# Latent attention: where the two short groups of context queries stand in each set of heads

## The reference, cut to what matters

```
def block_attention(q, k, v, scale):
    ...
    def one_block(qi):
        s = jnp.einsum('bhqd,bhkd->bhqk', qi, k).astype(jnp.float32) * scale
        p = jax.nn.softmax(s, axis=-1).astype(v.dtype)
        return jnp.einsum('bhqk,bhkd->bhqd', p, v)
...
a_lat = block_attention(qa_l, jnp.concatenate([ka_c, ka_l], axis=2), jnp.concatenate([va_c, va_l], axis=2), scale)
...
y_ctx = combine(block_attention(qa_c, ka_c, va_c, scale), h_c, mo_c, z_c, u_ctx.dtype)
```

## Time and profile before

| | |
|---|---|
| median of 3 executions | 4053.97 us (4051.37 to 4055.36) |
| profiled execution, its own time | 4052.3 us |
| its span | 4050.5 us |
| mean granted TensorE clock | 0.989 |
| TensorE busy | 3951.8 us (98%) |
| VectorE, ScalarE, GpSimd busy | 44%, 24%, 21% |
| the attention, first score maximum to last output | 304.22 to 674.16 us |
| first instruction of the next stage on TensorE | 674.95 us |

### The profile page before, as it was taken

The page is one execution under the profiler, slowest core; times in us unless marked ns, Lnnn a source line. Parts: engine busy times, 40 slices in busy tenths (PEclk is TensorE's granted clock), DMA queues, the critical chain, the costliest instruction groups (busy, mean ns, idle before and its releaser), DMA issues. The chain is left out here.

```text
span 4050.5 us, 48141 instructions
## 1 busy us (share of the span) xinstructions
PE 3951.8 (98%) x18490; PEld 2440.7 (60%) x18490; DVE 1775.2 (44%) x3770; ACT 957.0 (24%) x1802; POOL 835.2 (21%) x911
## 2 busy tenths in 40 slices
PE   7999999999999999989999999999999999999998
PEld 4688886877558468567544565656544444444447
DVE  3227775577333366646356322222523252223134
ACT  4223332333114311155225311111111010000001
POOL 0006665101111111132012112123100022111223
PEclk8999999999999999999999999999999999999999
DMA  5320003110202121132131112113243101111113
GB/s 212 125 91 8 8 9 64 47 44 34 102 28 77 50 63 48 58 109 94 47 95 50 57 36 80 41 57 104 94 184 104 52 32 42 42 42 48 46 42 104
DMA packets 113571, 270.24 MB, mean 67 GB/s; under 512 B 15479, under 2 KB 45033, under 8 KB 112254
## 3 DMA queue, kind: packets, MB, share of 16 engines
q1 hardware_dynamic: 106368, 251.81, 18.8%
q0 software_dynamic: 5920, 13.25, 1.4%
q10 hardware_dynamic: 1056, 2.10, 0.1%
HBM read 218.53 MB, written 50.87 MB: 67 GB/s over the span
## 5 line engine op out<-in xcount | busy, mean ns | idle before, releaser
L426 PE MATMUL upper_banks<-sbuf 128*128 128x512 f32 (+1 forms) x2016 | 771.4, 545 | 1.5 <-issue 1.1
L3152 PE MATMUL upper_banks<-sbuf 128*128 128x512 f32 x1400 | 614.6, 595 | 5.6 <-ACT sbuf L3411 3.9
L426 PEld LDWEIGHTS upper_banks<-sbuf 128*128 128x128 f32 x2016 | 382.4, 190 | 388.7 <-issue 374.2
L3152 PEld LDWEIGHTS upper_banks<-sbuf 128*128 128x128 f32 x1400 | 262.7, 191 | 316.5 <-issue 307.0
L2417 PE MATMUL gla_prod<-sbuf 128*128 128x512 f32 x560 | 247.6, 593 | 0.3 <-DVE sbuf L2449 0.3
L378 POOL TENSOR_TENSOR sbuf<-sbuf 128x512 f32<-128x512 f32 x36 | 47.7, 1325 | 901.8 <-POOLq L68 330.0
L582 DVE TENSOR_TENSOR sbuf<-upper_banks,sbuf 128x512 f32<-128x512 f32 (+1 forms) x140 | 81.9, 585 | 283.1 <-PE upper_banks L426 282.6
L1007 PE MATMUL mla_banks<-sbuf 128*128 128x128 f32 x1344 | 175.2, 279 | 12.1 <-DVE sbuf L1314 8.5
L2417 PEld LDWEIGHTS gla_prod<-sbuf 128*128 128x128 f32 x560 | 104.5, 192 | 119.9 <-issue 117.4
L1007 PEld LDWEIGHTS mla_banks<-sbuf 128*128 128x128 f32 x1344 | 162.7, 194 | 21.8 <-issue 11.6
L1627 PE MATMUL mls_banks<-sbuf 128*128 128x512 f32 x392 | 175.1, 593 | 0.0
(11 more groups left out here) (535 smaller groups left out, 6497.2 us busy)
## 6 DMA issues: line engine op xcount, KB each, us to landing
sbuf<-in_l_w_in SPq DMA_DIRECT2D x59, 512.0 KB, 4.0
sbuf<-in_w_in SPq DMA_DIRECT2D x52, 512.0 KB, 4.4
sbuf<-in_w_mlp_out SPq DMA_DIRECT2D x40, 512.0 KB, 3.6
sbuf<-in_w_mlp_in SPq DMA_DIRECT2D x32, 512.0 KB, 3.6
sbuf<-in_l_w_mod SPq DMA_DIRECT2D x24, 512.0 KB, 5.2
scratch_gates<-sbuf SPq DMA_DIRECT2D x48, 256.0 KB, 2.0
sbuf<-scratch_gates SPq DMA_DIRECT2D x8, 1536.0 KB, 6.8
sbuf<-in_l_w_mod SPq DMA_DIRECT2D x8, 1024.0 KB, 15.3
```

Source lines behind the costliest of these rows:

```text
L426: last = nc.tensor.matmul(bank_of(n, c)[:, 0:wd], lw[:, k * P:(k + 1) * P], right_operand(c, base, tw, k, o, wd, to), start=k == 0 and c i ...
L3152: last = nc.tensor.matmul(pb, lw[:, k * P:(k + 1) * P], rhs, start=k == 0 and c in ("P1", "P2", "P5"), stop=k == 3, skip_group_check=True)
```

## The change

In each of the first three sets the order of query tiles becomes 2 3 4 0 5 6 7 1 8 9; in the last it becomes 2 3 4 0 5 6 7 8 9 1. Before it was 2 to 9 and then 0 and 1 in all four. The number of groups, their content and all formulas for waits stay; those that count by the group's kind (`nkt`, `adds`) follow the list.

```
-    groups = [(j, t) for j in range(4) for t in list(range(2, TT)) + [0, 1]]
+    groups = [(j, t) for j in range(4) for t in ((2, 3, 4, 0, 5, 6, 7, 1, 8, 9) if j < 3 else (2, 3, 4, 0, 5, 6, 7, 8, 9, 1))]
```

## The result

The changed kernel takes 4076.05 us (median of 6, 4073.26 to 4082.04), the kernel before 4052.67 us in the same comparison (median of 6, 4049.48 to 4055.36). Ratio 1.0059, 95% interval 1.0046 to 1.0072: 23.4 us slower. The forecast was 4073, slower, between 4064 and 4081.

What follows compares the result with a forecast made beforehand. Long groups were taken as bound by TensorE's work plus small waits, nearly matched by GpSimd's two-group chain, with GpSimd ending last in the first short group. 4052.3 + 16.1 + 3.0 = 4071.4, 4073 against the median; range 4064 to 4081.

Steps and rivals of the forecast that it cites:

- Long to short: First layer's attention: time from a long group's first VectorE score maximum to the next short group's, claimed to stay 8.82 us.
- Short to long: First layer's attention: time from a lone short group's first VectorE score maximum to the next long group's, claimed 10.40 us.
- The long step behind: First layer's attention: step from the long group after a lone short one to the next long group, claimed 9.57 us.
- The sum at equal clock: First layer's attention, first marker to end, without new clock falls: 386.02 us against 369.94, claimed +16.1 us.
- The end: First layer's attention, from the last group's marker to the stage's end: claimed 11.78 us with one short group there.
- The mechanism: Inside a lone short group, GpSimd's key sums for the long neighbour hide its work; it costs 9.60 us, like a long one.
- The clock: TensorE in lone short groups: one in three falls to the lower clock, two falls of 1.52 us, claimed +3.0 us.
- clock falls at most of the places: Rival for TensorE at the seven lone short groups: five to seven falls of 1.52 us, 4076 to 4079 us, chance 0.20.
- The signs of being wrong: Short-to-long step under 8 us, GpSimd's long key sums starting under 7.3 us after the marker, or later stages moving over 2 us.
- Hidden shorts: Rival in first layer's attention: long neighbours fill TensorE's idle time, lone short group costs 5.85 us, about 4042 us, chance 0.05.
- Half hidden: Rival in first layer's attention: GpSimd starts the next long group earlier, shrinking long steps from 9.62; about 4056 us, chance 0.06.

Runs made afterwards that it cites:

- all three traces: The changed kernel traced three times with nothing altered: first trace's profiled span 4074.1 us, second run 4075.94 us, third 4074.90 us.
- the grouping that goes the other way: Against the kernel before, all eight short groups in one run behind the 32 long ones: 4037.63 us, ratio 0.9960; ahead of them: 4038.24 us, ratio 0.9954.

## Why the prediction was right, and by how much

*Steps.* Long to short 8.82 forecast, 8.81 to 8.82 in all eight places. Short to long 10.40 forecast, 10.38 to 10.40 in three places at the higher clock. The one of 10.68 came in all three traces at the same place, with GpSimd's late start. The long step behind: 9.57 forecast, 9.57 or 9.58 in the five places without a fall.

*The sum at equal clock.* 386.02 forecast. Measured 393.89 less 1.63, 1.64, 1.63, 1.62 and 1.61 (the five falls, each a step less its usual length) and 0.28 (the late rotation) is 385.48; with the late rotation left in, 385.76. The 24 other long steps took 230.11 where I had 230.88: between lone short groups there are only two or three of them, and the first ones are at 9.57 to 9.58. The end took 12.07 where I had 11.78; its clock was 0.69 and the weighing of the long group ahead already ran partly at the lower level, so that the sum over keys came 5.60 us after the marker in place of 5.31.

*The mechanism* was right, and incomplete in its words. I named one place, GpSimd's key sums, and wrote that a lone short group's work is hidden behind them. Taking them away gave 1.92 us a place, not the 3.75 between 10.40 and the 6.65 of a short group behind a short one. TensorE stands idle at three places of every boundary: entering the short group, inside it, and in the long group behind. The sum held because it was made from pieces of the trace, which carry all three, not from the cause.

*The clock* is the term that was mis-sized. Forecast: two falls of 1.52, 3.0 us. Measured: five falls, 8.1 us, in the first trace. That is the rival "clock falls at most of the places" (4076 to 4079, chance 0.20), and 4076.05 is its lower end. Two things failed. The rate came from three pairs with one fall; and I looked only inside the short group, while two of the five falls came in the long step behind it, behind waits of 0.89 and 0.79 us that stood in the trace of before as well. That the price of a fall is about 1.5 was right (1.61 to 1.64 measured).

*Luck.* Counted from before's own time the forecast was +19.1 us (16.1 and 3.0), and the medians differ by 23.4. That 4076.05 lies 3 and not 4 us above 4073 is luck: the median of before came out at 4052.67 in this comparison, 1.3 under the 4053.97 that I started from. The equal-clock term, too high by 0.5, also hid a little of the clock's error.

*The signs of being wrong.* None came: the short-to-long step is over 10 us, what stands behind the stage moved by 0.2 us, and GpSimd began the key sums of the long group ahead 370.09 - 362.80 = 7.29 us after its marker, as before (378.81 - 371.52). Two slips of working changed nothing: a lone short group would have had to cost 7.3 us for no change (16.1 over seven places below 9.60), not 7.4; and the upper bound, 4079 + 1.7 with one or two more, is 4082 or 4083 and not 4081.

*The rivals.* Hidden shorts (4042) is out: its point was a start of the scores 3.75 us earlier, and TensorE waits for line 850 at all seven places. Even with GpSimd's sums cut the step was 8.48, not 6.65. The Trainium skill, "Perfetto Trace Analysis", section "Optimization Strategy", says that interleaving stretches with different most-contended engines may improve performance. Here the interleaving lost 23.4 us, and the grouping that goes the other way gained 0.4%. But TensorE is the busiest engine in both kinds (12.61 of 15.26 us and 65.3 of 67.3), so this case doesn't meet the rule's condition and says nothing against it; I had applied it to two kinds that differ in what TensorE waits for, not in the busiest engine. Half hidden is out too: the steps behind are 9.57.

*The difference as a whole,* in the two traces: at equal clock 385.48 - 368.42 = 17.1, falls 8.1 - 1.5 = 6.6, the late rotation 0.3, the stage's earlier start -0.6, all behind it +0.2: 23.6 us.

## What to carry to other kernels

When groups of two kinds go through one software pipeline, cost the boundaries between the kinds, not the groups. Work of the long neighbour that trails by one group on another engine (here 6.8 us of GpSimd's sums) fills the short group's slot, and scattering the short ones pays for it each time; here that was 2.1 of the 4.7 us a set, and waits for VectorE were 1.2 more. A table of steps by ordered pair of kinds isn't enough, because the chain is two groups long: short to long takes 6.65 us behind a short group and 10.40 behind a long one, and short to short 8.61 behind a long group and 5.08 behind a short one. The trace of before held only the 6.65, which is the rival at 4042. What gave the stage to 0.6 us in 386 at equal clock was to follow the releasing engine through the group and to join two pieces of the trace at the point where it lets TensorE go. The falls of the clock, 8.1 us here, are in no such sum. Then put like beside like: inside one run of eight a short group took 5.08 us, where a lone one cost 9.6.

## What was not expected of the hardware

TensorE's granted clock fell to the lower of its two levels (1.2 in place of 2.4 GHz; 0.85 or 0.86 as the mean over a step) behind waits of TensorE of 0.7 to 1.1 us, five times in the stage of 394 us, each worth 1.6 us. Such waits stand at all seven places of a lone short group, and at two of the seven, in the first trace, neither the short nor the long step had a fall; what decides between them is open. It stayed at the higher level through five short groups (621.29 to 646.69 us, clock 1.00) whose matmuls come in many small pieces with waits of 0.16 us, once 0.29.
